# A two-layer backbone with a mixture of experts: experts' places read from a table by rank, 42 and 24 units instead of 44 and 26, further units in two long turns instead of eight short ones

## The chip, the cores and the metric

One core of a Trainium2 chip runs the whole program. The metric is the device time of one execution in microseconds (us); before and after are compared by the medians of their runs. The engines are TensorE (PE; PEld is its loading of the stationary operand), VectorE (DVE), ScalarE (ACT), GpSimd (POOL) and the sync engine (SP), which issues most transfers.

## The reference

Two layers work on 256 context tokens and 256 latent tokens of width 1024. Each layer has a mixing part (attention, neighbourhood attention, a long convolution), and then a mixture of experts, which is what the change touches:

```python
    _, eidx = lax.top_k(jnp.where(emask, sel, -jnp.inf), TOP_K)      # TOP_K = 8 of N_EXPERTS = 64
    wsel = jnp.take_along_axis(scores, eidx, -1)
    wsel = wsel / jnp.sum(wsel, -1, keepdims=True) * ROUTED_SCALE
    gate = jnp.sum(jax.nn.one_hot(eidx, N_EXPERTS, dtype=F32) * wsel[..., None], 1)
    a = jnp.einsum('td,edh->teh', h, w1)
    b = jnp.einsum('td,edh->teh', h, w3)
    act = (jax.nn.silu(a) * b * gate[..., None].astype(h.dtype))
    routed = jnp.einsum('teh,ehd->td', act, w2)
```

An expert has two matrices of 1024 x 128 (w1, w3) and one of 128 x 1024 (w2), in float32. Layer 0 routes all 512 tokens (4096 choices of an expert), layer 1 only the 256 latent tokens (2048 choices).

How many tokens choose each expert depends on the data alone. The reference, evaluated on its own inputs, gives these counts, in ascending order (rank 0 is the rarest expert):

```
layer 0: 26 27 27 30 | 31 33 36 37 38 38 38 38 40 41 42 42 42 43 44 45 46 47 49 50 53 56 57 61 62 62 | 64 65 66 66 68 70 70 70 70 70
         72 72 73 73 76 78 80 82 83 84 84 85 85 86 88 88 89 89 | 92 97 108 115 118 | 139
layer 1: 5 6 7 7 10 10 11 11 12 14 15 16 16 17 18 19 19 21 22 22 23 23 23 24 24 24 25 25 26 27 27 28 28 28 29 32 |
         33 33 34 35 35 35 36 38 39 40 40 42 44 44 44 45 47 48 49 50 50 54 55 60 | 77 78 79 90
```

The bars stand where the changed kernel's classes change (below).

## The kernel before

A *unit* is 128 token rows that go through the experts' products together. Its rows are cut in four *strips* of 32. `CLASSES` gives for each layer how many groups of each shape there are and how many strips each of their experts has: `QUAD` is one unit for four experts with a strip each, `PAIR` one unit for two experts with two strips each, `FOUR_IN_THREE` three units for four experts with three strips each, `SINGLE` one unit for one expert. Experts are placed in ascending order of their counts, so a rank decides an expert's class, its first strip (`base`) and its number of strips (`cap`). What does not fit in an expert's strips goes to an overflow unit. In layer 0 one overflow unit always stands in the sequence (`ALWAYS`, at the tenth group of `ALWAYS_AT`), with its own load of its expert's weights; further overflow units run behind the sequence in a loop `Fori(0, EXTRA_TURNS)` of 8 turns with 4 units each, under an `If` that reads their number at run time. By the counts above, the layouts of before have 172 strips (43 units) in layer 0 with one expert over its strips (139 tokens in 128 rows, so 11 in the overflow unit), and 104 strips (26 units) in layer 1 with none over.

`sequence(l)` mixes the classes evenly and holds three PAIR groups back for the end of layer 0. For each unit `n`, in program order on the engines:

- POOL: `gather` fetches the unit's token rows from DRAM by an index column, three units ahead (`AHEAD`), line 2571. In layer 0 `scatter` sends the unit's output rows to DRAM (L2584); in layer 1 PE sums them into PSUM instead (`combine`, L1393).
- SP: for each expert in order, `load_w13` (two transfers, w1 and w3) and two experts later `load_w2` (one transfer), from line 673 by way of L795 and L804. Eight experts' places form a ring (in the tiles `weights`, `features_h`, `qkv`, `a_q`, `probs_T` and `filters`); a load waits until the unit that used the place eight experts before is done.
- PE: `products` (L1361), the second half of the unit before (L1382, `second` with h = 1; in layer 1 `combine` there), `act_T` (L1369), `tokens_T` of the next unit (L1350), `second` with h = 0 (L1382), which waits for w2.
- ACT: SiLU of each unit (L1684) and copies; DVE: the product with the other factor, copies.

Each engine, SP too, has its own copy of the loop for further units behind its sequence. Every instruction in it is written out for the units of one turn, and an engine jumps over them where the `If` is false.

Before the units start, DVE works out each expert's rank and place (L2195 to L2240), PE adds and spreads them with small matmuls, SP waits for the list of experts in rank order (`list_ready`), and one-hot products make the index columns, whose width is `BLOCKS[l]` (79 and 62). Behind layer 0, POOL waits for all scatters (L2621), raises `y_sent` (L2622), and SP loads the rows back (`a_q<-scratch_y`) for layer 1. Behind layer 1, PE closes its sums (L1444) and DVE makes the last normalisation.

## Time and profile before

| | us |
|---|---|
| median of 3 runs | 1394.36 |
| lowest and highest run | 1391.6, 1397.8 |
| span of the profiled execution, first to last instruction | 1391.5 |
| PE busy, share of the span | 1234.7, 89% |
| DVE busy, share of the span | 606.4, 44% |

The profile names no device time of its own execution, only its span, so the sum in the prediction is made against the span and then set against the median of the runs, which is 2.9 us above the span; the span is within 0.1 us of the lowest run. Engines are busy at the same time; their shares don't add up. DMA share is the mean busy share of the core's 16 DMA engines, GB/s what they moved, PEclk TensorE's granted clock as a share of full speed.

### The profile page before, as it was taken

To read this page: it belongs to the slowest core of one execution; us is meant where nothing else is said; L and a number is where in the kernel's file an instruction comes from. 1 tells how busy PE (TensorE), PEld (TensorE's weight loads), DVE (VectorE), ACT (ScalarE), POOL (GpSimd) and SP (SyncE) were. 2 spreads that over 40 slices of the span, in tenths; PEclk is the share of its full clock that TensorE was granted. 3 is DMA by queue.
4 is the path that set the end of the run, shared out by engine and by line. 5 is a ranking of instruction groups with operands and counts; after the bars stand their busy time and mean duration, and the time that the engine had idled before them with its cause. 6 is when DMAs were issued, how large, how long until landed. Compare 5 with 4: busy or idle time off the path is not lost.

```text
span 1391.5 us, 20651 instructions
## 1 busy us (share of the span) xinstructions
PE 1234.7 (89%) x7127; PEld 649.2 (47%) x7127; DVE 606.4 (44%) x1421; ACT 282.8 (20%) x691; POOL 285.9 (21%) x370
## 2 busy tenths in 40 slices
PE   5899999898979999989879599999987798989893
PEld 1443445344444565555545344485543453545451
DVE  5312633546576222222222129175366543534355
ACT  0100114233211222222212211114411111111110
POOL 1000004235114233323332200104502210111010
PEclk9999999999989999999999799999997999999996
DMA  9965507745327999999999495433124999999960
GB/s 332 345 246 208 181 0 207 270 172 200 134 89 303 344 396 410 395 385 385 387 404 396 190 366 221 159 129 88 34 106 139 407 407 407 401 406 387 409 258 31
DMA packets 111361, 373.39 MB, mean 268 GB/s; under 512 B 16250, under 2 KB 22652, under 8 KB 103064
## 3 DMA queue, kind: packets, MB, share of 16 engines
q1 hardware_dynamic: 89112, 313.50, 59.6%
q0 software_dynamic: 21280, 55.39, 10.7%
q10 hardware_dynamic: 864, 3.15, 0.6%
q8 instruction: 60, 0.98, 0.3%
q14 instruction: 45, 0.37, 0.1%
HBM read 365.62 MB, written 27.33 MB: 282 GB/s over the span
## 4 chain that ended last, share of the span: by engine, by line
PE 50%; SPq 13%; DMA 10%; DVE 5%; issue 4%; ACT 2%; POOL 1%; POOLq 0%; DVEq 0%; ACTq 0%
SPq L673 10%; PE bank L1361 10%; PE bank L1382 6%; PE bank L1171 6%; DMA qkv<-in_exp_w 5%; PE bank L1393 4%; PE bank L969 3%; PE bank L1214 2%; PE bank L1350 2%; PE bank L977 2%; PE bank L1143 2%; PE bank L1157 2%; PE bank L1062 1%; PE bank L1052 1%; SPq L804 1%
## 5 line engine op out<-in xcount | busy, mean ns | idle before, releaser
L1361 PE MATMUL bank<-weights,b_qk 128*32 128x256 f32 (+2 forms) x1264 | 173.5, 395 | 8.8 <-DMA features_h<-in_exp_w 7.1
L1361 PEld LDWEIGHTS bank<-weights,b_qk 128*32 128x32 f32 (+2 forms) x1264 | 110.0, 137 | 73.0 <-issue 43.2
L1382 PE MATMUL bank<-weights,expert_act_T 128*32 128x512 f32 (+2 forms) x316 | 99.5, 633 | 17.5 <-DMA qkv<-in_exp_w 11.6
L2329 DVE TENSOR_TENSOR expert_act<-silu_a,bank 128x128 f32<-128x128 f32 x44 | 12.7, 288 | 212.6 <-ACT silu_a L1684 212.6
L1361 PE MATMUL bank<-features_h,b_qk 128*32 128x256 f32 (+2 forms) x688 | 103.9, 393 | 0.1
L2571 POOL DMA_INDIRECT shift_scale_gate_norm<-scratch_h,gather_index x76 | 78.6, 1034 | 67.7 <-POOL gather_index L2568 62.3
L1171 PE MATMUL bank<-weights,features_h 128*128 128x512 f32 x192 | 85.9, 603 | 0.7 <-ACT features_h L1471 0.7
L1350 PE MATMUL bank<-tab,shift_scale_gate_norm 128*128 128x128 f32 x576 | 76.5, 276 | 7.2 <-DMA shift_scale_gate_norm<-scratch_h,gather_index 7.2
L2524 POOL TENSOR_SCALAR probs<-probs,prob_recip 128x512 f32<-128x512 f32 (+1 forms) x36 | 48.4, 1353 | 165.1 <-DVE prob_recip L2052 165.0
L1684 ACT ACTIVATE silu_a<-bank 128x128 f32<-128x128 f32 x70 | 19.4, 278 | 294.5 <-PE bank L1361 294.5
L2319 DVE COPY b_qk<-bank 128x512 f32<-128x512 f32 x72 | 49.8, 692 | 58.5 <-PE bank L1350 58.5
L1350 PEld LDWEIGHTS bank<-tab,shift_scale_gate_norm 128*128 128x128 f32 x576 | 70.1, 191 | 10.8 <-issue 8.5
L1393 PE MATMUL bank<-tokens_h,a_k 128*128 128x512 bf16 x208 | 73.5, 394 | 0.8 <-DVE tokens_h L2337 0.8
L1361 PEld LDWEIGHTS bank<-features_h,b_qk 128*32 128x32 f32 (+2 forms) x688 | 56.7, 125 | 27.4 <-issue 14.3
L2524 POOL TENSOR_SCALAR tokens_h<-tokens_h,prob_recip 128x512 f32<-128x512 f32 (+1 forms) x36 | 49.5, 1384 | 88.5 <-DVE prob_recip L2052 88.5
L1361 PE MATMUL bank<-qkv,b_qk 128*64 128x256 f32 (+1 forms) x352 | 67.6, 387 | 0.0
L1382 PE MATMUL bank<-qkv,expert_act_T 128*32 128x512 f32 (+2 forms) x172 | 60.6, 647 | 7.4 <-DMA qkv<-in_exp_w 5.0
L1361 PE MATMUL bank<-a_q,b_qk 128*64 128x256 f32 (+2 forms) x336 | 62.4, 382 | 0.0
L1052 PE MATMUL bank<-features_h,weights 128*128 128x512 f32 (+1 forms) x192 | 62.4, 486 | 0.0
L1471 ACT ACTIVATE b_qk<-bank 128x512 f32<-128x512 f32 x76 | 45.4, 597 | 74.6 <-PE bank L1350 62.1
L977 PE MATMUL bank<-weights,features_h 128*128 128x512 f32 x128 | 58.1, 611 | 2.6 <-ACT features_h L1521 2.6
L2568 POOL COPY gather_index<-token_of_slot 128x1 int32<-128x1 int32 x76 | 15.7, 207 | 212.6 <-PE bank L1350 205.4
(364 smaller groups left out, 2024.7 us busy)
## 6 DMA issues: line engine op xcount, KB each, us to landing
weights<-in_exp_w SPq DMA_DIRECT2D x195, 512.0 KB, 13.8
features_h<-in_exp_w SPq DMA_DIRECT2D x64, 512.0 KB, 11.7
qkv<-in_exp_w SPq DMA_DIRECT2D x64, 512.0 KB, 15.9
shift_scale_gate_norm<-in_ada_w SPq DMA_DIRECT2D x24, 1024.0 KB, 7.9
a_q<-in_exp_w SPq DMA_DIRECT2D x32, 512.0 KB, 12.6
weights<-in_w_in SPq DMA_DIRECT2D x6, 2048.0 KB
shift_scale_gate_norm<-scratch_mod POOLq DMA_DIRECT2D x16, 512.0 KB, 9.2
c_padded<-in_ada_w SPq DMA_DIRECT2D x8, 1024.0 KB, 6.0
```

The lines of the kernel that those rows point to most:

```text
L673: sp.dma_start(dst, src).then_inc(s, inc)
L977: mm = pe.matmul(b[:, :], HT[:, k, t * P:(t + 1) * P], w[:, k, :], start=k == 0, stop=k == KD - 1)
L1052: mm = pe.matmul(b[:, first:HALF], w[:, k, (f % 4) * P:(f % 4 + 1) * P], HT[:, k, first:HALF], start=k == 0, stop=k == KD - 1)
L1171: mm = pe.matmul(b[:, :], OT[:, c, t * P:(t + 1) * P], wo[:, c, :], start=c == 0, stop=c == KD - 1)
L1350: mm = pe.transpose(XT_PS[k // 4][:, (k % 4) * P:(k % 4 + 1) * P], XG[:, u.slot(), k:D:KD], ident)
L1361: mm = pe.matmul(ab[r, 0:2 * HIDDEN].rearrange("p (m h) -> p m h", m=2), XGT[:, u.slot() % 2, k, r], expert_w13(slot)[:, :, k, :], start=k ...
L1382: mm = pe.matmul(yp[h][r, :], ACTT[:, r], expert_w2(slot)[:, h * HALF:(h + 1) * HALF], start=True, stop=True)
L1393: mm = pe.matmul(ACC[g][h][:, :], GROW[:, u.slot() % 2, g * P:(g + 1) * P], part[u.slot() % 2][:, h * HALF:(h + 1) * HALF], start=False, s ...
L1471: return nc.scalar.activation(dst, src, ACT.Copy)
L2319: dve.tensor_copy(XGT[:, u.slot() % 2, 4:8, :], XT_PS[1][:, :].rearrange("p (k t) -> p k t", k=4)).then_inc(L["xT_vector"], 1)
L2524: pool.tensor_scalar(P_[U % 4][:, 0:nk], P_[U % 4][:, 0:nk], RC[:, U % 4:U % 4 + 1], None, ALU.mult).then_inc(p_ready, 1)
L2571: nc.gpsimd.indirect_dma_start(out=XG[:, v, :], out_offset=None, in_=h_dram, in_offset=bass.IndirectOffsetOnAxis(ap=IDXB[:, v:v + 1].bitca ...
```

## The change

Layer 0 now has 1 QUAD, 13 PAIR, 7 FOUR_IN_THREE, 5 SINGLE and 1 `DOUBLE` group (one expert in two units, eight strips), which are 42 units; the standing overflow unit and its load are gone. Layer 1 has 9 QUAD, 12 PAIR and 1 FOUR_IN_THREE, which are 24 units. By the counts above no expert of either layer is over its strips; in layer 1 the expert of rank 35 has 32 tokens in 32 rows, all other experts of both layers have 2 rows or more to spare.

An expert's first strip and the end of its strips are now read from a table by its rank (`starts`, built by `strip_starts`), in place of arithmetic with two bounds. Further units run in 2 turns of 24 (layer 0) and 20 units (layer 1), in place of 8 turns of 4. Index columns are wider (`BLOCKS` 94 and 68 in place of 79 and 62), and some constants share one table (`iota`). `FORCED` is empty in both layers, so it does nothing.

```diff
-CLASSES = (((15, PAIR, 2), (6, FOUR_IN_THREE, 3), (10, SINGLE, 4)),
-           ((8, QUAD, 1), (14, PAIR, 2), (4, SINGLE, 4)))
+DOUBLE = SINGLE * 2
...
-ALWAYS = (1, 0)
-ALWAYS_AT = 10
+def strips_of(shape):
+
+    return 4 * len(shape) // experts_of(shape)
+
+
+FORCED = ((), ())
+CLASSES = (((1, QUAD), (13, PAIR), (7, FOUR_IN_THREE), (5, SINGLE), (1, DOUBLE)),
+           ((9, QUAD), (12, PAIR), (1, FOUR_IN_THREE)))
...
 LAST_PAIRS = (3, 0)
-SHARE = (32, 32)
+PAIRS = 1
+UNITS = tuple(sum(n * len(shape) for n, shape in classes) for classes in CLASSES)
+SHARE = 32
...
-EXTRA = 32
-EXTRA_TURNS = EXTRA // UNROLL
+EXTRA_TURNS = 2
+EXTRA_UNITS = (24, 20)
+EXTRA = tuple(EXTRA_TURNS * n for n in EXTRA_UNITS)
 AHEAD = 3
-BLOCKS = tuple(n + EXTRA + UNROLL for n in UNITS)
+BLOCKS = tuple(n + m + UNROLL for n, m in zip(UNITS, EXTRA))
 BLOCKS_MAX = max(BLOCKS)
-LISTED = EXPERTS + EXTRA + UNROLL
+LISTED = tuple(EXPERTS + n + UNROLL for n in EXTRA)
+LISTED_MAX = max(LISTED)
...
+def strip_starts(l):
+
+    starts = [0]
+    for n, shape in CLASSES[l]:
+        starts += [starts[-1] + strips_of(shape) * (k + 1) for k in range(n * experts_of(shape))]
+    assert len(starts) == EXPERTS + 1 and starts[-1] == 4 * UNITS[l]
+    return starts
...
-        if at == ALWAYS_AT:
-            for n in range(ALWAYS[l]):
-                seq.append((UNITS[l] + n, [(x, EXPERTS + n, slice(0, P))]))
-                x += 1
...
-                loads = EXPERTS + ALWAYS[l]
+                loads = EXPERTS
...
-                        if where[x] >= EXPERTS:
-                            sp.wait_ge(list_ready, 2 * l + 2)
...
-                more = pe.value_load(LIST[0:1, LISTED:LISTED + 1], min_val=0, max_val=EXTRA)
+                more = pe.value_load(LIST[0:1, LISTED[l]:LISTED[l] + 1], min_val=0, max_val=EXTRA[l])
+                each = EXTRA_UNITS[l]
                 with pe.Fori(0, EXTRA_TURNS) as i:
-                    with pe.If(i * UNROLL < more):
-                        for c in range(every, every + UNROLL):
-                            u = At(i, c)
-                            slot, fills = c - every, i + (-(-(EXPERTS + ALWAYS[l] - (c - every)) // ring_n) + 1)
+                    with pe.If(i * each < more):
+                        for c in range(every, every + each):
+                            u = At(i, c, each)
...
-                one, (two, four) = CLASSES[l][0][2], BOUNDS[l]
-                more_two, more_four = CLASSES[l][1][2] - one, CLASSES[l][2][2] - CLASSES[l][1][2]
-                count, key, rank, cap, base, over, upto, t0, t1, t2, t3 = (NB1[0:EXPERTS, i:i + 1] for i in range(11))
+                count, key, rank, base, end, over, upto, t1, t2 = (NB1[0:EXPERTS, i:i + 1] for i in range(9))
                 b = filled(("count", l))
-                iota = const("iota_slot")[0:EXPERTS, 0:EXPERTS]
+                iota = const("iota")[0:EXPERTS, 0:EXPERTS]
                 KEY, ALL1 = RT[0:EXPERTS, 7, 0:EXPERTS], RT[0:EXPERTS, 7, 64:64 + EXPERTS]
+                key_row = const("key_row")[0:EXPERTS, l * EXPERTS:(l + 1) * EXPERTS]
+                starts = const("starts")[0:EXPERTS, l * (EXPERTS + 1):(l + 1) * (EXPERTS + 1)]
                 free(dve.memset(ALL1, 1.0))
+                free(ts(key, b[0:EXPERTS, 0:1], float(EXPERTS), const("key")[0:EXPERTS, l:l + 1], ALU.mult, ALU.add))
                 free(ts(count, b[0:EXPERTS, 0:1], 1.0, None, ALU.mult))
-                drained(("count", l), stt(KEY, b[0:EXPERTS, 64:64 + EXPERTS], float(EXPERTS), iota, ALU.mult, ALU.subtract))
+                drained(("count", l), stt(KEY, b[0:EXPERTS, 64:64 + EXPERTS], float(EXPERTS), key_row, ALU.mult, ALU.add))
                 dve.wait_ge(vector_step, steps[0])
-                link(ts(key, count, float(EXPERTS), const("iota_expert")[0:EXPERTS, :], ALU.mult, ALU.subtract))
                 link(stt(RT[0:EXPERTS, 7, 128:128 + EXPERTS], KEY, key, ALL1, ALU.is_lt, ALU.mult, accum_out=rank))
-                free(ts(t0, rank, two - 0.5, float(more_two), ALU.is_gt, ALU.mult))
-                free(ts(t1, rank, four - 0.5, float(more_four), ALU.is_gt, ALU.mult))
-                free(ts(t2, rank, -float(two), 0.0, ALU.add, ALU.max))
-                link(ts(t3, rank, -float(four), 0.0, ALU.add, ALU.max))
-                free(stt(cap, t0, float(one), t1, ALU.add, ALU.add))
-                free(ts(base, rank, float(one), None, ALU.mult))
-                link(ts(t2, t2, float(more_two), None, ALU.mult))
-                link(stt(t3, t3, float(more_four), t2, ALU.mult, ALU.add))
-                link(tt(base, base, t3, ALU.add))
-                link(stt(t2, cap, -float(SHARE[l]), count, ALU.mult, ALU.add))
+                free(stt(RT[0:EXPERTS, 7, 192:192 + EXPERTS], iota, rank, starts[:, 0:EXPERTS], ALU.is_equal, ALU.mult, accum_out=base))
+                free(stt(RT[0:EXPERTS, 7, 128:128 + EXPERTS], iota, rank, starts[:, 1:EXPERTS + 1], ALU.is_equal, ALU.mult, accum_out=end))
+                dve.wait_ge(vector_step, steps[0])
+                link(stt(t2, end, -float(SHARE), count, ALU.mult, ALU.add))
+                link(stt(t2, base, float(SHARE), t2, ALU.mult, ALU.add))
...
-                link(tt(t3, cap, base, ALU.add))
-                free(ts(NB16[0:EXPERTS, 256:320], ident[0:EXPERTS, 0:EXPERTS], t3, None, ALU.mult))
+                free(ts(NB16[0:EXPERTS, 256:320], ident[0:EXPERTS, 0:EXPERTS], end, None, ALU.mult))
...
-                turns = LIST[0:1, LISTED:LISTED + 1]
-                free(ts(turns, b[0:1, LISTED - EXPERTS:LISTED - EXPERTS + 1], float(UNROLL - 1 - ALWAYS[l]), float(EXTRA), ALU.add,
-                        ALU.min))
+                free(ts(LIST[0:1, EXPERTS:LISTED[l]], b[0:1, 0:LISTED[l] - EXPERTS], float(EXPERTS - 1), None, ALU.min))
+                turns, more_at = LIST[0:1, LISTED[l]:LISTED[l] + 1], b[0:1, LISTED[l] - EXPERTS:LISTED[l] - EXPERTS + 1]
+                free(ts(NB1[0:1, 9:10], more_at, 0.5, float(EXTRA_UNITS[l]), ALU.is_gt, ALU.mult))
+                free(ts(NB1[0:1, 10:11], more_at, EXTRA_UNITS[l] + 0.5, float(EXTRA_UNITS[l]), ALU.is_gt, ALU.mult))
...
-                link(ts(turns, turns, int(math.log2(UNROLL)), None, ALU.logical_shift_right))
-                link(ts(turns, turns, int(math.log2(UNROLL)), None, ALU.logical_shift_left))
+                link(tt(turns, NB1[0:1, 9:10], NB1[0:1, 10:11], ALU.add))
```

**What stands in another place in the program.** On DVE, in layer 0 (layer 1 has the same rows), this is the chain from the experts' counts to the overflow (`block_counts` holds one number for each expert, `c_padded` 64 x 64 work tiles, `tab` the constants). Before:

```order
L2199 TENSOR_SCALAR block_counts<-block_counts,tab 64x1
L2200 SCALAR_TENSOR_TENSOR c_padded,block_counts<-c_padded,block_counts 64x64
L2201 TENSOR_SCALAR block_counts<-block_counts 64x1
L2202 TENSOR_SCALAR block_counts<-block_counts 64x1
L2203 TENSOR_SCALAR block_counts<-block_counts 64x1
L2204 TENSOR_SCALAR block_counts<-block_counts 64x1
L2205 SCALAR_TENSOR_TENSOR block_counts<-block_counts 64x1
L2206 TENSOR_SCALAR block_counts<-block_counts 64x1
L2207 TENSOR_SCALAR block_counts<-block_counts 64x1
L2208 SCALAR_TENSOR_TENSOR block_counts<-block_counts 64x1
L2209 TENSOR_TENSOR block_counts<-block_counts 64x1
L2210 SCALAR_TENSOR_TENSOR block_counts<-block_counts 64x1
```

and after the change:

```order
L2220 SCALAR_TENSOR_TENSOR c_padded,block_counts<-c_padded,block_counts 64x64
L2221 SCALAR_TENSOR_TENSOR c_padded,block_counts<-tab,block_counts 64x64
L2222 SCALAR_TENSOR_TENSOR c_padded,block_counts<-tab,block_counts 64x64
L2224 SCALAR_TENSOR_TENSOR block_counts<-block_counts 64x1
L2225 SCALAR_TENSOR_TENSOR block_counts<-block_counts 64x1
L2226 TENSOR_SCALAR block_counts<-block_counts 64x1
```

The multiply that made the key is no longer a step of its own behind the counts (it stands further up, beside other free ones), and ten steps on one column each behind the rank (the second row of before, the first of after) have become two 64 x 64 lookups and two steps on a column; the last row of after is the test for overflow, which before is the row behind the last one shown (L2211).

On PE, this is where layer 1's loop for further units begins, behind the last `combine`: before,

```order
L1393 MATMUL bank<-tokens_h,a_k 128x512
L1427 TENSOR_LOAD block_experts
L1427 ISA x2
L1428 UNCONDITIONAL_BRANCH
L1428 ISA
L1429 COMPARE_AND_BRANCH
```

and after,

```order
L1411 MATMUL bank<-tokens_h,a_k 128x512
L1445 TENSOR_LOAD block_experts
L1445 ISA x2
L1447 UNCONDITIONAL_BRANCH
L1447 ISA
L1448 COMPARE_AND_BRANCH
```

and where it ends, before,

```order
L1393 MATMUL bank<-residual,a_k 128x512
L1393 MATMUL bank<-tokens_h,a_k 128x512
L1429 UNCONDITIONAL_BRANCH
L1428 REGISTER_ALU
L1428 COMPARE_AND_BRANCH
L1444 MATMUL bank<-count_tables 128x512 x4
```

and after,

```order
L1411 MATMUL bank<-residual,a_k 128x512
L1411 MATMUL bank<-tokens_h,a_k 128x512
L1448 UNCONDITIONAL_BRANCH
L1447 REGISTER_ALU
L1447 COMPARE_AND_BRANCH
L1464 MATMUL bank<-count_tables 128x512 x4
```

The rows of the branches are the same. What moved is the distance: before, 73 rows of four units lie between the first compare and the branch back, after, 357 rows of twenty units, and every row of matmuls is jumped over where no further unit is needed. On POOL in layer 0 the same loop follows the last scatter (`TENSOR_LOAD` reads the number of further units), before,

```order
L2581 COPY scatter_index<-choice_of_slot 128x1
L2584 DMA scratch_y<-tokens_h,scatter_index 4096x1024
L2609 UNCONDITIONAL_BRANCH
L2609 ISA
L2610 COMPARE_AND_BRANCH
```

and after,

```order
L2595 COPY scatter_index<-choice_of_slot 128x1
L2598 DMA scratch_y<-tokens_h,scatter_index 4096x1024
L2623 UNCONDITIONAL_BRANCH
L2623 ISA
L2624 COMPARE_AND_BRANCH
```

with 35 rows of four units behind it before and 195 rows of 24 units after.

## Rows read from the trace of the kernel before

**Rows 1.** The page: span, busy time, and ACT's SiLU, one a unit.

```profile
span 1391.5 us, 20651 instructions
...
PE 1234.7 (89%) x7127; PEld 649.2 (47%) x7127; DVE 606.4 (44%) x1421; ACT 282.8 (20%) x691; POOL 285.9 (21%) x370
...
L1684 ACT ACTIVATE silu_a<-bank 128x128 f32<-128x128 f32 x70 | 19.4, 278 | 294.5 <-PE bank L1361 294.5
```

**Rows 2.** Busy time by stretch: layer 0's units, layer 1's units; then PEclk, DMA share, GB/s.

```profile
458.00:783.00 325.00, 299.70 (x2377) 174.61 (x2373) 80.56 (x197) 75.54 (x173) 102.77 (x168) 0.96 0.98 378
1097.00:1358.00 261.00, 242.19 (x1762) 122.83 (x1759) 119.15 (x201) 44.03 (x101) 28.64 (x48) 0.97 0.97 382
```

**Rows 3.** All loads of experts' weights: who waited longest for them (us, times).

```profile
  PE bank L1382: 34.5, 14
```

**Rows 4.** DMA issues: times, size of one, median us to landing.

```profile
weights<-in_exp_w SPq DMA_DIRECT2D x195, 512.0 KB, 13.8
```

**Rows 5.** Timeline of ACT, two SiLUs of neighbouring units of layer 0: start, us.

```profile
512.60 0.28 ACT L1684 ACTIVATE silu_a<-bank 128x128 f32<-128x128 f32 x1 [3.04 <-PE bank L1361]
519.31 0.28 ACT L1684 ACTIVATE silu_a<-bank 128x128 f32<-128x128 f32 x1 [3.11 <-PE bank L1361]
```

**Rows 6.** The chain that ended last, layer 0, two loads: start, us, what.

```profile
710.89 19.99 DMA qkv<-in_exp_w
...
760.34 17.24 DMA probs_T<-in_exp_w
```

**Rows 7.** The same chain in layer 1, pieces on PE.

```profile
1246.35 1.47 PE bank L1382 x8
...
1311.29 1.56 PE bank L1382 x8
...
1344.45 3.59 PE bank L1361 x64
...
1350.48 0.99 PE bank L1382 x8
...
1353.91 3.60 PE bank L1361 x32
```

**Rows 8.** Timeline of DVE, layer 1, key to overflow test.

```profile
1065.02 0.20 DVE L2199 TENSOR_SCALAR block_counts<-block_counts,tab 64x1 f32<-64x1 f32 x1
1065.26 0.28 DVE L2200 SCALAR_TENSOR_TENSOR c_padded<-c_padded,block_counts 64x64 f32<-64x64 f32 x1
...
1065.58 0.14 DVE L2201 TENSOR_SCALAR block_counts<-block_counts 64x1 f32<-64x1 f32 x1
...
1066.62 0.15 DVE L2210 SCALAR_TENSOR_TENSOR block_counts<-block_counts 64x1 f32<-64x1 f32 x1
1066.81 0.15 DVE L2211 TENSOR_SCALAR block_counts<-block_counts 64x1 f32<-64x1 f32 x1
```

**Rows 9.** The chain behind layer 1's last unit, PE's loop for further units.

```profile
1367.18 5.48 issue
```

**Rows 10.** Timeline of ACT behind layer 0's last unit; in brackets the idle time before.

```profile
789.80 2.44 ACT L1472 ACTIVATE probs_T<-tab,choice_gates 128x128 f32<-128x128 f32 x8 [3.80 <-issue]
```

**Rows 11.** The chain behind layer 0's last unit: POOL's loop, then `y_sent`.

```profile
787.95 0.03 POOLq L2609
...
791.50 0.04 POOLq L2609
...
792.09 0.03 POOLq L2622
```

**Rows 12.** DMA from 786 to 793 us in 40 slices of 0.175 us.

```profile
GB/s 0 0 0 0 351 374 445 398 398 304 374 117 0 94 0 0 0 0 0 0 0 304 398 398 374 445 421 351 211 0 0 0 0 0 0 0 0 0 0 0
```

**Rows 13.** PE's instruction queue, whole span, then 1367 to 1373 us: packets, MB, share.

```profile
q8 instruction: 60, 0.98, 0.3%
...
q8 instruction: 1, 0.02, 1.0%
```

**Rows 14.** DMA issues: a small transfer, on the queue of SP.

```profile
cond<-in_cond SPq DMA_DIRECT2D x1, 8.0 KB, 2.8
```

168 lines of the change are left out of this document (88 added, 80 removed).

## The prediction

> **What bounds the kernel now.** First the page: 70 SiLUs are the 44 and 26 units of the sequences and nothing more [rows 1], so no turn for further units was taken. Then busy time by stretch, for the two runs of units that fill 42% of the span [rows 2]: PE is busy 92 and 93% of them, but the DMA engines 98 and 97%, at 378 and 382 GB/s. Both are near their limit, so it matters which one the other waits for. All loads of experts' weights show PE waiting for them 34.5 us in 14 waits in `second` alone [rows 3]: the loads come last. The timeline agrees: where nothing is late a unit of layer 0 takes PE 6.71 us (519.31 - 512.60) [rows 5], so 43 steps between the first and the last SiLU are 289 us, and the stretch holds 325. In layer 1 a unit takes 9.46 us (1353.91 - 1344.45) [rows 7]. The chain of work gives the loads' own pace. In layer 0 the w2 that PE waits for landed at 730.88 for the place `qkv` (710.89 + 19.99; by the ring the 54th expert loaded) and at 777.58 for `probs_T` (760.34 + 17.24; the 63rd) [rows 6]: 5.19 us an expert. In layer 1 PE went on at 1246.35 with the 38th expert's w2, and at 1311.29 with the 53rd's [rows 7]: 4.33 us an expert.
>
> **Layer 0's units: -4.1 us.** Two units fewer would be 13.4 us of PE, but PE waits for loads up to 777.58, five us before the stretch ends. What shortens the stream is the one expert load that goes, the overflow unit's: three transfers of 512 KB [rows 4], 1.57 MB, at 378 GB/s 4.16 us. The rows gathered and scattered stay 4096 each, since they are the choices. Bounds: nothing, if the new order, which has its FOUR_IN_THREE groups earlier and a QUAD (four experts at once) in the middle, lets the DMA engines stand idle as long; 5.2 us, the pace of an expert with its share of gathers. I take 4.1: the rings refill long before the end.
>
> **Layer 1's units: -0.8 us in place of 18.9.** 24 units bring the same 64 experts. In the new sequence the last group of four, the 59th to the 62nd expert, stands one unit before the end, as before, so its `second` waits for the 62nd's w2, and what follows it is the same. By the pace that w2 lands at 1311.29 + 9 x 4.33 = 1350.3. Before, PE came to that same `second` at 1350.48 [rows 7], by its own pace, since its last wait lay four units back. So fewer units bring 0.2 us. The rest is the stream's start: the chain of small steps on DVE. The key's multiply, 0.24 us (1065.26 - 1065.02), goes; the steps from the rank to the overflow test took 1.23 us (1065.58 to 1066.81), ten of them; two lookups of the rank's own kind take 0.32 us each (1065.58 - 1065.26) and two linked steps 0.19 each (1066.81 - 1066.62) [rows 8], which is 1.02. Together -0.45, and the link for `t3` behind it -0.19: 0.6 us, so the first load starts 0.6 us earlier. Bounds: 0 to 4.
>
> **Layer 0's start: 0.** The same 0.6 us is saved there, and given back by index columns 94 wide in place of 79: their one-hot products and PE's 32 matmuls on them grow by a fifth. The other added or dropped rows (constants, a memset, a wait of SP for `list_ready` that was long over) lie behind loads and matmuls. What they cost without that cover is tenths of a us.
>
> **The loops for further units.** Eight turns became two. POOL's turn takes 0.44 us (791.50 - 787.95, by eight) [rows 11]; ACT's eight with the read of their number are 3.80 us [rows 10], so the read is some 0.2. PE's eight are 5.48 us [rows 9], 1.7 more than ACT's, and in that gap one packet of PE's instruction queue lands [rows 13]. Without any cost for code, two turns are 0.2 + 0.9 = 1.1 us, so PE saves 4.4 behind layer 1, where its loop is on the chain.
>
> But code has to be there to be run. PE's queue brought 60 packets of 0.98 MB, 16.3 KB each, in the whole span [rows 13], for 14,254 matmuls and weight loads [rows 1]: 69 bytes each, which is the whole program once, with next to nothing there at the start. A unit of the loop in layer 1 is written as 31 matmuls (8 in `products`, 1, 8, 2 and 12), the ten on float32 weights run twice, each with a weight load: 82 instructions, 5.7 KB. Four are 23 KB, 1.4 packets; twenty are 113 KB, seven packets. A jump over seven packets goes to code that has not been fetched. One fetch's price: the 1.7 us by which PE's gap exceeds ACT's, with one packet in it; no less than 0, if PE's turns are slow by themselves, and at most the 2.8 us of the small 8 KB transfer [rows 14]. How many: the jump forward misses; whether the head of the loop is still held when PE jumps back, no row shows. Is it not, then there are three (forward, back, forward). PE's gap is then 1.1 + 3 x 1.7 = 6.2 us, +0.7; with one fetch 2.8, -2.7.
>
> POOL's loop in layer 0 is the second on the chain: `y_sent` at 792.09 [rows 11]. Its 24 units are some 316 instructions as built, 20 KB in place of 4. Beside it the last scatter is under way, whose data move until 786 + 29 x 0.175 = 791.1 [rows 12], so shorter turns win at most 0.9 us here (I take 0.5), and one fetch is hidden: 787.95 + 0.9 + 0.6 + 1.7 = 791.2. With three it is 794.6, +2.5. The loops of ACT, DVE and SP have work or waits beside them: the rows of layer 1's first gathered results arrive later than ACT's diagonals, and DVE waits for PE's sums at the end.
>
> The Trainium skill ("Runtime: NRT & Kernel Launch", Instruction fetch mechanics) says that instructions come in blocks of 16 KiB, and that a taken branch to a target outside a window of two pages waits for a DMA fetch of that page. The size of the packets here agrees with it (16.3 KB), the stall itself no row here shows. It speaks against the change: by it both jumps and the jump back miss, the case of three fetches. The sum without it would be the case without fetches.
>
> **The sum, likeliest case (three fetches of 1.7 us in both loops).** -4.1 - 0.8 + 0 + 0.7 + 2.5 = -1.7 us on the span of 1391.5; the median of the runs is 2.9 us above the span, 1394.4, and moves with it: **1392.7 us**.
>
> **The rivals.**
> - *One fetch a loop:* -4.1 - 0.8 - 2.7 - 0.5 = -8.1: 1386.3. For it: eight turns before brought only one packet, so something of the passed code is held. Against it: then the jump spanned 1.4 packets, now seven.
> - *No fetch counts:* -4.1 - 0.8 - 4.4 - 0.5 = -9.8: 1384.6. For it: PE fetched through the units with no wait seen. Against: there it runs straight on.
> - *PE is what bounds:* 2 x 6.71 + 2 x 9.46 = 32.3 us less: about 1362. For it: PE busy 92%. Against it: the waits, and DMA share 98% [rows 2, 3].
> - *Slower: an expert over its strips.* Rank 35 of layer 1 has exactly 32 tokens in 32 rows. A 33rd, from one token routed differently by rounding, makes one overflow unit, and the `If` then runs all 20 units: at least 20 x 9.46 = 189 us, about 1583. It decides from one token on; in the reference the narrowest choice of layer 1 is between two other experts.
> - *Slower by less:* fetches of 2.8 us, three a loop: PE +4.0, POOL +5.8, so +4.9 in all, 1399.3; slower by over 0.5% needs another 2 us.
> - *The table does nothing:* not possible, since the number of units follows from it.
>
> **How the numbers follow.** 0.5%, about what a measurement of this kernel can tell from no change, is 7 us. Chances: three fetches 0.50, of which 0.06 dearer than above; one fetch 0.20, in which -8.1 passes 7 us in two cases of three; none 0.15; PE bound, in whole or part, 0.05; the new order costs the stream some us 0.07, a few of them over 7; an expert over its strips 0.03. Faster by over 0.5%: 0.13 + 0.14 + 0.05 = 0.32; slower: 0.06 + 0.03 + 0.03 = 0.12; within: 0.56. The range takes in no fetch below and three dear ones above: 1384 to 1400.
>
> **What would show it.** 66 SiLUs. Layer 0's last one about 4 us earlier, layer 1's about 5, with PE still waiting for weights, in layer 1 now at its last group of four. The gap behind layer 1's last `combine`: about 6 us if three fetches, 3 if one, 1 if none; `y_sent` the same way. PE's instruction packets: ten or so more if the passed code is fetched in order, about the same as before if it is left out. More than 66 SiLUs would be the overflow. The forecast is wrong if that gap is short, or if both stretches shrink by whole units.

## The result and the profile after

Two measurements of the changed kernel, each against runs of the kernel before beside it:

| | changed, us | before, us | ratio, 95% interval |
|---|---|---|---|
| first | 1376.95 (6 runs, 1375.83 to 1384.26) | 1393.88 | 0.9901 [0.9872, 0.9929] |
| again | 1381.6 (11 runs, 1376.23 to 1386.37) | 1391.67 | 0.9931 [0.9910, 0.9952] |

The ratios say that the change made the kernel faster by 0.7 to 1.0%, some 10 to 14 us (the medians of the first measurement lie 16.9 us apart, those of the second 10.1). The forecast was 1.7 us, within a range of 1384 to 1400. The profiled execution took 1381.32 us, its span is 12.1 us shorter than the one before.

The page, then busy time in the two stretches of units (us, busy time by engine, PEclk, DMA share, GB/s):

```profile
span 1379.4 us, 20656 instructions
...
L1704 ACT ACTIVATE silu_a<-bank 128x128 f32<-128x128 f32 x66 | 18.3, 277 | 291.6 <-PE bank L1379 291.6
```

```profile
458.00:777.00 319.00, 289.86 (x2499) 162.40 (x2501) 76.56 (x187) 71.90 (x165) 98.91 (x161) 0.94 0.98 384
1090.00:1347.00 257.00, 224.42 (x1815) 108.23 (x1835) 109.55 (x185) 40.48 (x93) 26.24 (x44) 0.95 0.98 386
```

There are 66 SiLUs, as forecast. The DMA engines are as busy as in [rows 2], 98%, but they move 384 and 386 GB/s in place of 378 and 382. ACT's timeline has the first and the last SiLU of each layer:

```profile
461.93 0.28 ACT L1704 ACTIVATE silu_a<-bank 128x128 f32<-128x128 f32 x1 [4.54 <-PE bank L1379]
...
776.81 0.28 ACT L1704 ACTIVATE silu_a<-bank 128x128 f32<-128x128 f32 x1 [2.94 <-PE bank L1379]
...
1090.39 0.28 ACT L1704 ACTIVATE silu_a<-bank 128x128 f32<-128x128 f32 x1 [4.86 <-PE bank L1379]
...
1346.63 0.28 ACT L1704 ACTIVATE silu_a<-bank 128x128 f32<-128x128 f32 x1 [5.43 <-PE bank L1379]
```

I call the time from a layer's first SiLU to its last its *stretch*. Before, the four times were 458.97, 782.39, 1097.52 and 1357.57. The difference of the two spans, piece by piece:

| piece | before | after | difference | forecast |
|---|---|---|---|---|
| start to layer 0's first SiLU | 458.97 | 461.93 | +3.0 | 0 |
| layer 0's stretch | 323.42 | 314.88 | -8.5 | -4.1 |
| last SiLU to `y_sent` | 9.70 | 10.59 | +0.9 | +2.5 |
| from there to layer 1's first SiLU | 305.43 | 302.99 | -2.4 | -0.6 |
| layer 1's stretch | 260.05 | 256.24 | -3.8 | -0.2 |
| PE's gap behind the last `combine` | 5.48 | 4.32 | -1.2 | +0.7 |

The rest is equal. The +3.0 at the start lies ahead of everything that the change touches (PE reaches layer 0's router sums 2.9 us later already), and it belongs to the execution: four later variants with the same code there had their first SiLU at 457.0 to 458.1. The +0.9 behind layer 0 is of that kind too: the kernel before, profiled again (below), has 10.83 in place of 9.70.

The waits for experts' weights (us, times) show that PE waits for them as before, and more. After the change:

```profile
  PE bank L1400: 37.7, 14
  PE bank L1379: 17.4, 6
```

Before, `second` waited 34.5 us in 14 waits [rows 3]. The same view has those of `products`, which the forecast did not look at:

```profile
  PE bank L1361: 7.1, 3
```

So PE waited 41.6 us before and 55.1 after. PE's instruction queue brought 63 packets in place of 60 [rows 13], "about the same", which was the sign for passed code that is left out:

```profile
q8 instruction: 63, 1.03, 0.3%
```

PE's gap behind layer 1, and the chain behind layer 0's last unit (the wait for the last scatter, then `y_sent`):

```profile
1360.56 1.88 PE L1464 MATMUL bank<-count_tables 128*128 128x512 bf16 x4 [4.32 <-issue]
```

```profile
782.65 4.49 DMA scratch_y<-tokens_h,scatter_index
...
787.40 0.03 POOLq L2636
```

### The profile page after: what moved, and what is told of

Its sections match the earlier page's. It is cut to its first block, busy times and chain, and to the rows that moved or that the text cites. A ratio compares the mean times of both kernels' runs of the same rounds, so it can differ in the third digit from the quotient of the medians.

```text
span 1379.4 us, 20656 instructions
## 1 busy us (share of the span) xinstructions
PE 1204.2 (87%) x7284; PEld 620.8 (45%) x7307; DVE 594.2 (43%) x1388; ACT 276.0 (20%) x675; POOL 279.7 (20%) x358
## 2 busy tenths in 40 slices
DMA packets 110078, 371.94 MB, mean 270 GB/s; under 512 B 15338, under 2 KB 21740, under 8 KB 101768
## 4 chain that ended last, share of the span: by engine, by line
PE 48%; DMA 15%; SPq 10%; DVE 5%; issue 4%; ACT 2%; POOL 1%; POOLq 0%; DVEq 0%; ACTq 0%
PE bank L1379 11%; SPq L691 8%; PE bank L1189 6%; PE bank L1400 5%; DMA weights<-in_exp_w 5%; PE bank L987 3%; PE bank L1411 3%; DMA qkv<-in_exp_w 2%; PE bank L1232 2%; PE bank L1368 2%; PE bank L995 2%; PE bank L1175 2%; PE bank L1161 2%; PE bank L1080 2%; DMA c_padded<-in_ada_w 2%
## 5 line engine op out<-in xcount | busy, mean ns | idle before, releaser
L1379 PE MATMUL bank<-weights,b_qk 128*32 128x256 f32 (+2 forms) x1312 | 141.0, 398 | 13.3 <-DMA weights<-in_exp_w 10.5
L1379 PEld LDWEIGHTS bank<-weights,b_qk 128*32 128x32 f32 (+2 forms) x1312 | 82.6, 127 | 70.0 <-issue 42.3
L2342 DVE TENSOR_TENSOR expert_act<-silu_a,bank 128x128 f32<-128x128 f32 x42 | 12.1, 288 | 209.0 <-ACT silu_a L1704 209.0
L1379 PE MATMUL bank<-features_h,b_qk 128*32 128x256 f32 (+1 forms) x816 | 90.0, 394 | 2.6 <-DMA a_q<-in_exp_w 2.5
L1379 PE MATMUL bank<-qkv,b_qk 128*64 128x256 f32 (+2 forms) x336 | 83.5, 405 | 3.3 <-DMA weights<-in_exp_w 3.3
L2538 POOL TENSOR_SCALAR mod_rows_and_probs<-mod_rows_and_probs,prob_recip 128x512 f32<-128x512 f32 (+1 forms) x36 | 48.4, 1352 | 165.9 <-DVE prob_recip L2072 165.8
L2538 POOL TENSOR_SCALAR tokens_h<-tokens_h,prob_recip 128x512 f32<-128x512 f32 (+1 forms) x36 | 49.5, 1384 | 91.1 <-DVE prob_recip L2072 91.1
L1379 PEld LDWEIGHTS bank<-features_h,b_qk 128*32 128x32 f32 (+1 forms) x816 | 51.0, 124 | 36.8 <-issue 22.2
L1379 PE MATMUL bank<-a_q,b_qk 128*32 128x256 f32 (+2 forms) x368 | 66.4, 395 | 0.1
L1400 PE MATMUL bank<-qkv,expert_act_T 128*32 128x512 f32 (+1 forms) x204 | 51.7, 657 | 12.7 <-DMA qkv<-in_exp_w 6.8
L1379 PEld LDWEIGHTS bank<-qkv,b_qk 128*64 128x64 f32 (+2 forms) x336 | 46.0, 142 | 31.4 <-issue 18.8
L1400 PE MATMUL bank<-probs_T,expert_act_T 128*64 128x512 f32 (+2 forms) x84 | 48.1, 658 | 13.5 <-DMA weights<-in_exp_w 11.0
```

What stands on the lines that cost most here:

```text
L1379: mm = pe.matmul(ab[r, 0:2 * HIDDEN].rearrange("p (m h) -> p m h", m=2), XGT[:, u.slot() % 2, k, r], expert_w13(slot)[:, :, k, :], start=k ...
L1400: mm = pe.matmul(yp[h][r, :], ACTT[:, r], expert_w2(slot)[:, h * HALF:(h + 1) * HALF], start=True, stop=True)
L2538: pool.tensor_scalar(P_[U % 4][:, 0:nk], P_[U % 4][:, 0:nk], RC[:, U % 4:U % 4 + 1], None, ALU.mult).then_inc(p_ready, 1)
```

## The experiments

The theory after the result: loads do not run at a pace of their own; it depends on when places of the ring come free, so PE's units and the order of the groups count in part, and the loops cost one code fetch, not three. The rival is the forecast's: loads alone decide, and the missing us come from elsewhere (loops, DVE's chain).

### How much a difference between single profiles is worth

The kernel before and the changed one, each once more, unchanged.

> The kernel before once more, for a second profile of it. Both theories expect layer 0's stretch at 323.4 us and layer 1's at 260.0, within 1, and PE's gap behind the last combine at 5.48, since its code stands where it stood. If these scatter by more than that, the differences read from single profiles are worth that much less.

> The changed kernel itself once more, for its time beside the other runs of this chip and for a second profile of it. If the first SiLU at 461.93 us in its first profile (457.0 to 458.1 in three of the variants) was of that execution alone, it is at about 458 here, layer 0's stretch of SiLUs is again 314.9 within 1 us, layer 1's 256.2 within 1. Both theories expect the same here.

The kernel before: stretches of 322.46 and 260.04 us, PE's gap 5.42. The changed kernel: 314.88 and 256.98, gap 4.39; the first SiLU was at 460.86, so the expectation of 458 missed: that time varies with the execution, 457.0 to 463.1 over the variants without code of their own ahead of it. In the nine profiles with 42 units, eight places and all products in layer 0, whatever else differs (the kernel with the empty scatters, below, is not among them), its stretch is 314.5 to 315.8, mean 315.1. Layer 1's with 24 units is 254.4 to 260.3 in twelve, mean 256.7: read from single profiles, 2 us there mean nothing. So layer 0's stretch shrank by 7.8 us (322.9 to 315.1), layer 1's by about 3.3 (260.0 to 256.7).

From layer 0's last SiLU to `y_sent` the kernel before now takes 10.83 us, where it took 9.70, with the same code. Its last scatter took 5.01 us from issue to landing, and POOL's loop was through before it:

```profile
788.51 5.01 DMA scratch_y<-tokens_h,scatter_index
...
793.55 0.03 POOLq L2622
```

The changed kernel takes 10.59 and 10.54. Two profiles of each do not show that this piece got longer.

### Layer 0: the load and the two units

```diff
-CLASSES = (((1, QUAD), (13, PAIR), (7, FOUR_IN_THREE), (5, SINGLE), (1, DOUBLE)),
+CLASSES = (((0, QUAD), (15, PAIR), (6, FOUR_IN_THREE), (9, SINGLE), (1, DOUBLE)),
```

> The changed kernel with 44 units in layer 0 (15 PAIR, 6 FOUR_IN_THREE, 9 SINGLE, 1 DOUBLE, no QUAD); 64 experts are loaded once each and there is no overflow unit, all else as changed. Against the kernel before, this takes away the one load and no unit. Loads decide: first to last SiLU of layer 0 as in the changed kernel (314.9 us, within 1), the whole 1377. Rival, units count in part: the stretch shrank by 8.5 us where one load is worth 4.1, so the two units are worth the other 4.4: about 319, the whole 1381. Rival, the order with a QUAD in the middle costs something: the stretch gets shorter than 314.9.

Measured: 1383.48 us, ratio 0.9947 [0.9931, 0.9964]. Busy time from first to last SiLU, and the packets of this stretch:

```profile
457.50:776.20 318.70, 298.42 (x2365) 174.15 (x2367) 80.29 (x196) 75.27 (x172) 102.99 (x168) 0.96 0.98 379
```

```profile
DMA packets 36777, 120.94 MB, mean 379 GB/s; under 512 B 7329, under 2 KB 7329, under 8 KB 36743
```

The stretch is 318.7: 4.2 less than before with one load less, as forecast (4.1), and 3.6 more than with 42 units. The same line for the kernel before and for the changed one:

```profile
DMA packets 37243, 122.55 MB, mean 379 GB/s; under 512 B 7403, under 2 KB 7403, under 8 KB 37210
```

```profile
DMA packets 36196, 121.01 MB, mean 384 GB/s; under 512 B 6734, under 2 KB 6734, under 8 KB 36161
```

Without the load the stretch carries 1.6 MB less at the same 379 GB/s; with 42 units it carries the same bytes at 384. The forecast had nothing for these two units.

With 43 units and no QUAD (15 PAIR, 7 FOUR_IN_THREE, 5 SINGLE, 1 DOUBLE):

> The changed kernel with 43 units in layer 0 and no QUAD (15 PAIR, 7 FOUR_IN_THREE, 5 SINGLE, 1 DOUBLE); 64 loads. If the number of units sets the difference of 3.8 us between 44 (318.7) and 42 (314.9), by empty rows or otherwise, the stretch is 316.8 within 0.8. If it was the classes and their order (six groups of FOUR_IN_THREE and nine SINGLEs against seven and five), 43 units with seven groups and five SINGLEs are like 42: 314.9 or, since the QUAD holds four of the eight places at once, less.

317.5 us: between the two, just inside the first expectation. Nothing here says that the QUAD slows the changed kernel.

### Is it PE's work?

```diff
-                    for k in range(KD):
+                    used = range(KD) if summed else range(0, KD, 2)
+                    for k in used:
...
```

> The changed kernel with half of PE's products left out in layer 0's units (every second of the eight steps of the inner dimension, so the experts' first two products are not the reference's there); every load, gather and scatter stays. It makes PE's unit some 2 us shorter (about 80 us in all) and leaves the transfers alone. Loads alone decide: layer 0's stretch stays at 314.9 us within 2, with the waits grown by those 80 us. Rival, PE frees the places and so sets part of the pace: 121.0 MB at the 410 GB/s seen where nothing holds them up are 295 us, so the stretch falls to 295 to 300.

```profile
461.00:776.00 315.00, 231.17 (x1627) 115.49 (x1625) 76.35 (x186) 71.69 (x164) 97.88 (x160) 0.87 0.98 386
```

PE is busy 231 us in place of 286, and the stretch stays, 315.3. My theory of that moment (295 to 300) fell: with 42 units PE's work costs nothing, and the transfers do not reach 410 GB/s though PE frees the places early. The same cut in layer 1 (24 units), then in both layers with 44 and 26 units, then in the kernel before:

> The changed kernel with half of PE's products left out in layer 1's units (every second of the eight steps of the inner dimension, so layer 1's experts are not the reference's); loads and gathers stay. In layer 0 the same cut took 55 us off PE's busy time and left the stretch as it was (315.3 against 314.9). Loads alone decide in layer 1 too: 256.2 to 257.0 stay, within 1. Rival, PE's pace (9.46 us a unit, 24 x 9.46 = 227 of 256) sets part of it, which would make two units fewer worth the 3 us measured: the stretch falls by 5 us or more.

> The changed kernel with 44 units in layer 0 (15 PAIR, 6 FOUR_IN_THREE, 9 SINGLE, 1 DOUBLE) and 26 in layer 1 (8 QUAD, 14 PAIR, 4 SINGLE), and half of PE's products left out in both layers' units (so the experts' results are not the reference's); loads, gathers and scatters stay. With all products these layouts had stretches of 318.7 and 258.9 us, the changed ones 314.9 and 256.2 to 257.0, and halving the products left the changed ones as they were (315.3 and 256.7). If PE's units are what costs the 3.8 and the 2.5 us there, at 44 and 26 units but no more at 42 and 24, the stretches fall to 315 and 256.7. If it is the order, in which groups hold the places for weights, PE's share is nothing here either: 318.7 and 258.9 stay.

> The kernel before with half of PE's products left out in both layers' units (its results are not the reference's). Its stretches were 323.4 us (44 units, the 45th being no more than the overflow unit among them, 65 loads) and 260.0 (26 units). The overflow unit's load was worth 4.7 of the 8.5 us. If PE's units make the other 3.8, layer 0's stretch falls to 319.6 and layer 1's to about 257; if order does, they stay at 323.4 and 260.0 within 1.

Layer 0's stretch:

| layout | all products | half of them |
|---|---|---|
| before: 44 units, 65 loads | 323.4, 322.5 | 320.0 |
| 44 units, 64 loads | 318.7 | 317.8 |
| 42 units, 64 loads | 315.1 (nine) | 315.3 |

The kernel before, half of the products:

```profile
458.60:778.60 320.00, 238.63 (x1573) 123.45 (x1575) 80.27 (x196) 75.25 (x173) 103.11 (x168) 0.88 0.98 384
```

So PE's work cost 2.9 us before and nothing that shows with 42 units. The 0.9 with 44 units and 64 loads is a difference of two single profiles, where nine of one layout lie 1.3 us apart. Neither expectation of the last two runs is met whole: between 44 and 42 units, 2.5 of the 3.6 us stay where PE has some 55 us less to do (317.8 to 315.3). In layer 1 the stretch with half of the products is 259.1 before, 254.9 with 26 units and 256.7 with 24, as with all of them: within what single profiles scatter, the lengths alone tell no share of PE. The place at which PE waits does ("Why the forecast was wrong", layer 1's units).

### Is it the empty rows, or the places?

A unit moves 128 rows each way, and those without a choice leave small packets. One more indirect DMA a unit, of empty rows alone:

```diff
+                    if scatters:
+                        nc.gpsimd.indirect_dma_start(
+                            out=skip_dram, out_offset=bass.IndirectOffsetOnAxis(ap=IDXS[:, 0:1].bitcast(U32), axis=0),
+                            in_=TAB[:, 0:HALF], in_offset=None,
+                            bounds_check=P - 1, oob_is_err=False).then_inc(skipped, 16)
...
```

> The changed kernel with one more indirect DMA a unit in layer 0, 42 in all, behind each gather on POOL's queue: a scatter whose 128 indices all lie outside, so that it moves no row and leaves small packets alone (144 a transfer, 128 rows and 16 for the semaphore, as an empty half of a unit's gather or scatter does), some 6,050 more packets and no bytes. 44 units against 42 had 3.8 us more of layer 0's stretch at the same bytes (120.94 and 121.00 MB), and 576 small packets more. If those packets cost it (3.8 us x 16 engines / 576 = 0.106 us each), the stretch grows by 6,050 x 0.106 / 16 = 40 us, to 355. Rival, they cost what the profile shows for them, 9 ns: 3.4 us, to 318. Rival, something else of a unit made the 3.8: at most 3.4 us.

```profile
DMA packets 39391, 120.98 MB, mean 380 GB/s; under 512 B 9942, under 2 KB 9942, under 8 KB 39356
```

The stretch is 318.2: 3.1 us more, with 9,942 small packets where the changed kernel has 6,734 and, taken again, 6,775: some 3,170 more, half of what I had counted. If they alone make the 3.1 us, that is 3.1 x 16 / 3,170 = 16 ns each. This is the most they can be worth: each shows 9 ns in the trace, and POOL is busy 39 us longer (136.9 in place of 97.9) with issuing these transfers. The 576 packets of two units are then worth at most 0.6 us, a sixth of the 3.6. (The whole is longer still, 1392.6 us; POOL's loop, below, shows 8 us of it.)

Seven places of the ring in layer 0 in place of eight:

```diff
-RING_X = (8, 8)
+RING_X = (7, 8)
```

> The changed kernel with seven places for experts' weights in layer 0 in place of eight; the same 64 loads, the same units. Loads alone decide, with the DMA engines full either way (the forecast's reason): the stretch of layer 0 stays 314.9 us within 1. Rival, the loads run at 410 GB/s only while places are free, and PE frees them: one place fewer lowers the mean rate further below 384 GB/s, and the stretch grows by 3 to 15 us, with more waits for weights.

```profile
463.00:784.00 321.00, 287.47 (x2466) 161.06 (x2467) 76.33 (x186) 71.68 (x164) 97.88 (x160) 0.94 0.98 382
```

1384.84 us, ratio 0.9955 [0.9939, 0.9971]; the stretch is 321.2, 6.1 more for the same 64 loads and units. But it does not carry the same bytes:

```profile
DMA packets 36644, 122.65 MB, mean 382 GB/s; under 512 B 6782, under 2 KB 6782, under 8 KB 36609
```

That is 1.64 MB more than in the changed kernel, about one expert's weights (1.57 MB): with seven places one expert fewer is loaded before the first unit starts (9.73 in place of 11.36 MB on SP's queue up to the first SiLU). At 384 GB/s this alone is 4.3 us. The other 1.8 us are the rate, 382 in place of 384 GB/s. So the experiment shows first of all that a place is worth a load ahead of the units; that the number of places moves the pace, it shows by 1.8 us at most. The DMA share is 98% as ever, at 379 as at 386 GB/s, so the share does not tell the pace.

### Layer 1's two units

```diff
-           ((9, QUAD), (12, PAIR), (1, FOUR_IN_THREE)))
+           ((8, QUAD), (14, PAIR), (4, SINGLE)))
```

> The changed kernel with layer 1's old 26 units (8 QUAD, 14 PAIR, 4 SINGLE); all else as changed. Loads decide (the forecast's reason): both layouts load 64 experts, the last group of four stands one unit before the end in both, so two units more cost 0.2 us and the time stays within 1 us of the changed kernel's 1377.0. Rival, PE counts in part: the first to last SiLU of layer 1 took 3.8 us less with 24 units than with 26 before, so 26 bring 3 to 4 us back, 1380 to 1381. Rival, PE bound: 2 x 9.46 = 18.9 us, 1396.

1381.6 us, ratio 0.9932 [0.9910, 0.9954]; the stretch 258.9 (24 units: 256.7). That is 2.2 us, between the two expectations and at the edge of what one profile can tell. The whole time tells nothing: the changed kernel's ratios are 0.9901 and 0.9931. PE as the bound of the whole stretch (18.9 us) is out.

### The loops: turns, code, and where the code stands

```diff
-EXTRA_TURNS = 2
-EXTRA_UNITS = (24, 20)
+EXTRA_TURNS = 8
+EXTRA_UNITS = (4, 4)
...
```

> The changed kernel with the loops for further units as before: eight turns of four units (the index columns are as wide as before the change, or narrower). PE's gap behind layer 1's last combine was 5.48 us with eight turns of four and 4.32 with two of 24 and 20. If the loops are what changed there, the gap comes back to 5.5 (+1.2 us), and layer 0's POOL loop stays hidden behind the last scatter (4.5 us from issue to landing): about +1 us in all, 1378. If the loops have a share in more than that (the missing 11 us of the forecast), it is slower by more than 2 us.

> The changed kernel with two turns of four units: the turns of the change, the code of before (1.4 instruction packets of PE to jump over in place of seven); room for further units falls to eight, none is needed by the data. It tells code from turns in PE's gap behind layer 1: if turns alone count, 0.2 + 0.9 = 1.1 us; if one code fetch comes with the jump forward anyway, about 2.8; if the passed code does not matter, the 4.32 of the changed kernel. In all 0 to -3 us against the changed kernel. The index tables are 54 and 32 columns wide in place of 94 and 68, which may take some tenths off ahead of the units.

Eight turns: 1382.84 us, 0.9933 [0.9910, 0.9955]. Two turns of four units: 1378.58, 0.9897 [0.9873, 0.9922]; it has room for eight further units only. By the whole time neither can be told from the changed kernel (0.9901 [0.9872, 0.9929] and 0.9931 [0.9910, 0.9952]), so what follows is read from PE's gap. PE's timeline, both:

```profile
1359.55 0.60 PE L1464 MATMUL bank<-count_tables 128*128 128x512 bf16 x1 [8.46 <-issue]
```

```profile
1359.29 0.60 PE L1464 MATMUL bank<-count_tables 128*128 128x512 bf16 x1 [3.78 <-issue]
```

Eight turns took 8.46 us here, 5.48 before the change, with the same loop. To see whether the place of the code does this, 32 tiny matmuls went ahead of PE's first work:

```diff
+                    for _ in range(32 * (l == 0)):
+                        pe.matmul(b[0:FHID, 0:8], FW1[:, l, :], POS_SB[:, 0:8], start=True, stop=True)
```

> The kernel of the experiment with eight turns, with 32 tiny matmuls (128 PE instructions with their weight loads and second passes, about half of a 16.3 KB instruction packet) ahead of PE's first work, so that every later PE instruction stands 8 KB further on; nothing else is changed. PE's gap behind layer 1's last combine was 8.46 us with eight turns there and 5.48 with eight turns before the change. If where the loop stands in the packets decides, it moves away from 8.46 here, towards 5.5. If something else of the changed kernel made it 8.46 (longer code, other engines), it stays.

> The changed kernel with the same 32 tiny matmuls ahead of PE's first work as in the shifted kernel with eight turns, so that PE's code stands 8 KB further on. There the shift took PE's gap behind the last combine from 8.46 to 5.46 us. If two turns are as sensitive to the place, it moves by about 3 us from 4.32 here too; if they are not, since few turns can pay for it, it stays within 0.5 (it lay between 4.09 and 4.39 in the variants whose code before it was longer or shorter).

The gap is 5.46 us with eight turns, shifted, and 3.91 with two. (The start pays for the matmuls: the first SiLU is at 467.2 and 467.8.) The kernel before says the same without any shift: with half of its products left out, so with less code of PE ahead of the same loop of eight turns, its gap is 8.69 in place of 5.48. What differs is one branch. This is the line of the `If` on PE's queue, layer 1's loop alone (min/median/max ns, first and last start): the kernel before, the same with half of its products, eight turns, eight turns shifted, the changed kernel, each in a fence of its own.

```profile
L1429 PEldq COMPARE_BRANCH  x8: 214/221/350, 1366.5 to 1372.1; - x8
```

```profile
L1429 PEldq COMPARE_BRANCH  x8: 214/221/3623, 1355.3 to 1364.1; - x8
```

```profile
L1448 PEldq COMPARE_BRANCH  x8: 221/221/3378, 1350.5 to 1358.9; - x8
```

```profile
L1450 PEldq COMPARE_BRANCH  x8: 214/221/342, 1363.1 to 1368.7; - x8
```

```profile
L1448 PEldq COMPARE_BRANCH  x2: 221/2020/3820, 1355.6 to 1360.0; - x2
```

A branch over the units takes PE 0.22 us, and 3.3 to 3.9 where it waits. In layer 1 that happened once, at the first turn, or not at all: not in the kernel before (where the forecast saw a fetch of 1.7 us), nor in the shifted eight turns. That it waits for code is concluded from this dependence on the code's place; a packet of PE's instruction queue lands during the wait, but one lands in the gap without a wait too [rows 13]. In layer 0, where PE's loop is not on the chain, the wait is less regular: with the same code the kernel before shows a longest branch of 1.75 us in one execution and 3.90 in the other, and in the kernel with 43 units both turns waited, the second 6 us:

```profile
L1448 PEldq COMPARE_BRANCH  x2: 3777/5013/6249, 778.7 to 783.3; - x2
```

A turn without a wait takes PE 0.8 us (1366.5 to 1372.1 by seven), not the 0.45 of POOL and ACT. In all ten kernels with 24 and 20 units a turn, PE's gap is 3.9 to 4.4 us, of two turns with one wait.

POOL's branch behind layer 0 waits too: line 2624 is the `If`, line 2623 the end of a turn.

```profile
L2624 POOLq COMPARE_BRANCH  x2: 50/54/58, 782.6 to 786.1; - x2
```

```profile
L2623 POOLq ALU_OP  x2: 32/40/49, 785.6 to 786.4; - x2
```

From the first branch at 782.6 to the next instruction at 785.6 are 3.0 us; the second turn has no wait. In the kernel with two turns of four units the same step takes 0.1 us, and its last scatter lands 3.31 us behind its issue in place of 4.49. In the kernel with the empty scatters POOL waits four times in the same loop: at the first jump over the units, at the jump back, inside the loop's head (where nothing jumps), and at the second jump over the units. The chain of work:

```profile
784.59 3.35 issue
787.94 0.05 POOLq L2632
...
788.09 2.86 issue
790.94 0.05 POOLq L2632
790.99 2.31 issue
793.30 0.05 POOLq L2633
793.35 3.04 issue
```

These waits put `y_sent` 18.5 us behind the last SiLU, 8 us later than in the changed kernel, which is most of what this variant is slower by.

Without PE's loop in layer 1:

> The changed kernel without PE's loop for further units in layer 1 (the read of their number stays; the data need none of these units). PE's gap behind the last combine was 4.3 us with two turns over 20 units, 3.8 with two turns over four. If the forecast's price of a turn holds (0.45 us, the two 0.9) and the rest is the fetch of code behind the jump, the gap is the read alone, 0.2 to 0.5 us. If the read of the number or the wait for other engines makes part of it, more than 1 us stays.

PE's and DVE's timelines:

```profile
1357.14 1.03 PE L1464 MATMUL bank<-count_tables 128*128 128x512 bf16 x4
```

```profile
1360.93 1.29 DVE L2425 TENSOR_TENSOR qkv<-bank,shift_scale_gate_norm 128x512 f32<-128x512 f32 x2 [5.19 <-issue]
```

PE has no gap at all, though it still reads the number of further units, so the gap was the loop's. But from the last SiLU to the end of the span it is 30.9 us in place of 32.8, only 1.9 less: now DVE comes last, 5.19 us in its own copy of the loop, which PE's covered until then.

## Why the forecast was wrong

- **Layer 0's units, -4.1: the load was right, the nothing for the units was not.** The step that failed is "Two units fewer would be 13.4 us of PE, but PE waits for loads", from which the load alone was to shorten the stream. The load measures 4.2: 1.6 MB less at an unchanged 379 GB/s. The other layout of the 64 experts, with two units fewer, measures 3.6 more, since the same bytes went at 384 GB/s. I had divided the time by the experts loaded (5.19 us each) and taken the result for a property of the transfers. It is a mean over phases at 410 GB/s and phases at 320 to 390. GB/s in 40 slices of layer 0's stretch, before and after:

```profile
GB/s 350 386 320 335 390 414 412 408 405 407 411 413 400 391 405 396 395 361 411 359 394 359 385 400 392 383 401 394 365 404 404 393 412 401 400 385 405 398 233 78
```

```profile
GB/s 348 406 332 378 414 412 409 412 410 409 412 409 413 411 414 398 381 374 388 403 388 333 385 413 410 406 407 399 367 406 376 412 411 406 376 406 401 404 236 97
```

  Of all 7.8 us, 2.9 went by way of PE's work (nothing of that is left with 42 units); 2.2 are the load where PE is light, and 2.5 the layout there (the last 0.2 is 315.1 against 315.3), of which empty rows may be 0.6 at most. These parts are differences of single profiles, good to about 1 us, and the load is 4.2 or 2.2 by the company it keeps, so that it hit the forecast's 4.1 within 0.1 is luck in part. What in the order of groups makes the other 1.9 us is not shown. The places that groups hold are one candidate, and the experiment with seven places leaves room for it (1.8 us by the rate), but no run tests it.
- **Layer 1's units, -0.8: the chain was right, the -0.2 too small.** From the rank (L2200) to the overflow test took 1.55 us in [rows 8], and the multiply ahead of it 0.24; now it is 1.21 (L2220 to L2226 below), with no multiply: -0.58 against the 0.6 forecast.

```profile
1058.37 0.28 DVE L2220 SCALAR_TENSOR_TENSOR c_padded<-c_padded,block_counts 64x64 f32<-64x64 f32 x1
...
1059.58 0.15 DVE L2226 TENSOR_SCALAR block_counts<-block_counts 64x1 f32<-64x1 f32 x1
```

  The stretch gave 3.3 in place of 0.2. The step that failed is "By the pace that w2 lands at 1311.29 + 9 x 4.33 = 1350.3", from which PE and the load were to arrive together. The trace of before has the landing itself. SP issued the w2 of the 62nd expert at 1332.2, and it took 14.7 us:

```profile
L673 SPq DMA_DIRECT2D qkv<-in_exp_w x1: 362/362/362, 1332.2 to 1332.2; - x1
```

```profile
qkv<-in_exp_w SPq DMA_DIRECT2D x1, 512.0 KB, 14.7
```

  So it landed at 1346.9, and PE came to it at 1350.48 [rows 7], 3.6 us late, by its own pace over the last four units. With two units fewer PE comes in time and waits for the same load, in the chain of the changed kernel:

```profile
1325.05 14.19 DMA qkv<-in_exp_w
...
1339.48 1.06 PE bank L1400 x8
```

  Counted from the first SiLU, the load landed at 249.4 us before and at 248.9 after, so the stream's pace hardly moved, and PE went on at 253.0 before and at 249.1 after: these 3.9 us are the stretch's 3.8. The kernel with 26 units in layer 1 again has its last wait for weights four units before the end. That "PE waits for loads" did not hold for those last units, and there PE's units counted.
- **PE's loop, +0.7: measured -1.2.** The step that failed is the price: "the 1.7 us by which PE's gap exceeds ACT's, with one packet in it". The excess was PE's slower turns, 0.8 against 0.45 us, and no fetch. A real one costs 3.2 to 3.6 us here (3.38 and 3.82 less 0.22), and there is one, not three: neither the jump back nor the second jump forward waited. Six turns fewer give 4.8 us, the fetch takes some 3.6.
- **POOL's loop, +2.5: measured +0.9, and that is within what executions scatter.** The step that failed is the count of fetches again: one of 3.0 us, not three of 1.7, so POOL was through its turns at 786.4, before the last scatter landed (787.14). The kernel before has 9.70 and 10.83 in this piece, the changed one 10.59 and 10.54. Over all profiles there is a tendency: four more with the short code have 9.4 to 9.8, and all eleven with the long code (the empty scatters left out) 9.9 to 11.4; why the last scatter would land later there is not shown. More fetches in a row than the likeliest case had exist: in the kernel with the empty scatters.
- **Layer 0's start, 0: right.** From the count of tokens to the first SiLU it was 48.9 and 48.3 us before, 48.9 and 48.2 after. That the wider index columns take back what the chain saves shows where they are narrower: 47.5 us in the kernel with eight turns (78 columns), 47.1 in the one with 54.
- **The rest**, 1.1 us, are the execution's own +3.0 and -1.8.

The Trainium skill ("Runtime: NRT & Kernel Launch", Instruction fetch mechanics) says that a taken branch out of a window of two pages waits for a DMA fetch. The runs agree that a jump can cost a wait that depends on where the code stands, 2.6 to 3.6 us each in the loops on the chain. They disagree with counting one for each jump: in the changed kernel neither PE's way back over seven packets nor its second way forward waited in layer 1, and POOL's did not either, while another kernel's POOL waited each time.

## What to carry to other kernels

A DMA share of 98% with waits for loads does not make the loads a fixed pace: compare bytes and GB/s phase by phase. Where two things are to arrive together by an extrapolated pace, look up the landing in the trace: here PE was 3.6 us late for a load that the forecast had landing just ahead of it. When a ring gets a place less, look first whether a load has only moved into the stretch that is measured. Before pricing work "at nothing because something else waits", halve it in an experiment; here it was worth 2.9 us of 323 in one layout and 0 in another. A run-time loop that never runs costs microseconds on every engine that has a copy, several of them side by side: fewer turns make it smaller, a jump can put a wait of about 3 us into it, and taking it off PE alone gave 1.9 us of PE's 4.3, since DVE's copy then came last.

## What had not been expected of the hardware

- An empty turn costs PE 0.8 us where POOL and ACT take 0.45, and a jump costs nothing or, as a rule, 2.6 to 3.6 us by where the code stands (1.5 to 6.0 over all loops): 8 KB more code at the start of the program moved the end of one kernel's loop by 3.0 us (8.46 to 5.46).
- An indirect DMA whose 128 indices all lie outside left 80 small packets, not 144 (18,698 in the whole program in place of 15,338, by 42 transfers), and made the stretch longer by at most 16 ns of one engine for each.
- One more indirect DMA a unit made POOL's code longer, and its loop behind layer 0 then waited four times, 11.6 us together.
